# FFN entry: the rows of x turned by a product with a diagonal of the root, inside the last block of wo

## The chip, the cores and the metric

The kernel runs on one core of a Trainium2 chip. The metric is the device time of one execution in microseconds (us). The engines are named as in the profile: PE is TensorE (PEld its weight loads), DVE is VectorE, ACT is ScalarE, POOL is GpSimd, SP is SyncE, which issues every DMA here.

## The reference

One decoder layer on x of 256 tokens by 1024 channels, in float32. Three sub-layers follow each other, each wrapped in a norm before and a norm after:

```
h = rms_norm(x, norm_pre_xa)
y = cross_attention(h, rms_norm(mem, norm_mem), wq, wkv, wo)   # ends with o @ wo
x = x + rms_norm(y, norm_post_xa)
h = rms_norm(x, norm_pre_ffn)
y = (silu(h @ w_in[:, :2816]) * (h @ w_in[:, 2816:])) @ w_out
x = x + rms_norm(y, norm_post_ffn)
rms_norm(x, g) = x * rsqrt(mean(x * x) + 1e-6) * g             # mean over the 1024 channels
```

The change lies between `o @ wo` and the first products with the FFN's `w_in`.

## The kernel before

Float32 products with weights are made as three products each (`mm3`): an operand is split into a high part (rounded to a shorter format, written by ACT) and a rest (operand minus high, by DVE or POOL), and high by high, high by rest and rest by high are added up in one PSUM bank. Weights come in slots of 8 KB per partition; a slot is two halves, and half `i` is split by `high_part(act, i)` (ACT, line 344) and `rest(eng, e, i)` (DVE or POOL, line 350). A high part may be written only when the products with half `i - 4` are done, since there are four buffers for split halves. SP loads slot `n` when both rests of the slot that had its place before are made. On ACT, `highs(upto)` writes all high parts not yet written, up to half `upto - 1`; on DVE, `rests(upto)` does the same with rests. Before half `H_FIN` (the first FFN half, `first = 2 * S_FIN`) DVE makes all rests; from there on it makes the even halves, and POOL the odd ones. Below, "FFN half 0, 1, 2, 3" are `first` to `first + 3`: halves 0 and 1 are the gate's first 256 columns (channels 0 to 511, then 512 to 1023), halves 2 and 3 the up projection's.

Each engine works through its own instructions in the order of the program text, and semaphores tie them together. So the order of the calls in each engine's block is the order of the work.

wo is token-major (`split_token_major`): four PSUM banks, `wo0` and `wo1` for the first 128 tokens (block 0, columns 0 to 511 and 512 to 1023), `wo2` and `wo3` for the last 128 (block 1). Its 8 k-tiles are 8 weight halves, 12 products of 512 columns each. The first k-tiles run over all four banks; the last `last_kts` k-tiles run bank by bank, so that `wo0` is full first and `wo3` last.

For each block `m` of 128 tokens there follows a chain over three engines. ACT squares the two banks and makes the root (`post_root`), DVE multiplies the banks by the gain (`post_gain`) and adds them to x (`x_new`), ACT squares the new x and makes the root of the pre-norm (`pre_square`, `pre_part`, `pre_root`), DVE multiplies x by root and gain (`pre_norm`), PE turns the block by transposes (`turn_block`), and ACT and DVE split the turned block (`fft_high`, `fft_rest`). Then PE makes the first 256 gate and up columns block by block (`first_pair(m, e)`, where `e` is 0 for gate and 1 for up, 24 products each): turn 0, pair (0, gate), turn 1, pair (0, up), pair (1, gate), pair (1, up). After that come `g1`, `u1`, `g2` and so on for all 256 tokens at once, and the last product `y`.

The parts that the change touches, with what calls them:

Of the kernel before, what the change touches and what calls it, by code (L numbers as in the profile page):

```python
# [5 lines left out]
F32 = mybir.dt.float32  # L6
F32R = mybir.dt.float32r
ALU = mybir.AluOpType
# [72 lines left out]
H_WKV, H_LATE = 2 * S_WKV, 2 * S_WOUT  # L81
H_WQ, H_V7, H_WO, H_FIN = (2 * n for n in (S_WQ, S_V7, S_WO, S_FIN))
HALF_BUFS, MID_BUFS = 4, 2
Y_ORDER = [2, 3, 6, 7, 0, 1, 4, 5]

def trunk_kernel(nc, x_t, x_rows, mem_t, consts_d, params_d, weights_d, gains_d, rel_scratch, out):
    ctx = ExitStack()
    with ctx:  # L89
# [136 lines left out]
        act_split = [act_high, act_rest]  # L226
        fft = v3(own(ctx, "fft", 1024), 512)
        third_slot = own(ctx, "third_slot", SLOT)

# [3 lines left out]
        def cols(n):  # L233
# [22 lines left out]
            ml_row_step ml_den mb_inv s5_step2 rw_tail s5_sig x_inv f_sig s5_sq s5_root ml_sq  # L256
            ml_root rw_sq rw_root mb_sq mb_root
            w_high w_rest_even w_rest_odd w_rest_mid w_used high_ready act_rest y_rest h_high h_rest x_summed
# [108 lines left out]
        def _(pe):  # L367
# [46 lines left out]

            def split_token_major(first, tag, banks, act, order, last_kts, arrive, between=None):

# [19 lines left out]
                for m in range(2):  # L436
                    for half in range(2):
                        for kt in range(n - last_kts, n):
                            last = product(kt, m, half)
                            if m + half == 2 and kt < n - 1:  # L440
                                used(last, first + kt)
                        last.then_inc(full[banks[2 * m + half]], 1)
                half_user[first + n - 1] = f"{tag}3"
# [402 lines left out]

            split_token_major(2 * S_WO, "wo", (4, 5, 6, 7), ox_split, range(KD), 3, ox_arrives)

            def turn_block(m):

                for half in range(2):
                    i = 2 * m + half
                    o = v3(pe_open(pe, f"fft{i}", i)[:, :], P)
                    pe.wait_ge(S["xn_ready"], i + 1)
                    for k in range(4):
                        c = 4 * half + k
                        last = nc.tensor.transpose(o[:, k, :], xtmp[:, m, c * P:(c + 1) * P], const("ident"))
                    last.then_inc(full[i], 1)

            def first_pair(m, e):  # L860

                name = f"gu{m}"
                if e == 0:
                    pe_open(pe, name, 4 + m)
                o = bank[4 + m][:, 256 * e:256 * (e + 1)]
                for j in range(2):
# [11 lines left out]
                if e == 1:  # L878
# [82 lines left out]
        def _(pool):  # L961
# [76 lines left out]
            g.tensor_tensor(Sm[:, :, P:P + T], Sm[:, :, P:P + T], spread(mb_sum[:, 4:8], T), ALU.mult).then_inc(S["mb_prob"], 1)  # L1038
            for i in range(H_FIN + 1, NHALF, 2):
                rest(pool, g, i)  # L1040

        @block.scalar
        def _(act):
# [354 lines left out]
            pre_square(1, 0, 0)  # L1398
            pre_part(1, 0, 1.0 / D, "eps6")
            pre_square(1, 0, 1)  # L1400
            pre_root(1, 0, 1.0 / D)
            post_root(1, "wo", 1)
            highs(first + 2)

            def fft_high(m):
                for half in range(2):
                    o = v3(wait_full(act, f"fft{2 * m + half}")[:, :], P)
                    a.activation(h_split[0][:, 4 * half:4 * half + 4, m * P:(m + 1) * P], o,
                                 ACT.Copy).then_inc(S["high_ready"], 1)

            fft_high(0)
            pre_square(1, 1, 0)
            pre_part(1, 1, 1.0 / D, "eps6")
            pre_square(1, 1, 1)
            pre_root(1, 1, 1.0 / D)
            highs(first + 4)
            fft_high(1)

# [29 lines left out]
        def _(dve):  # L1448
# [10 lines left out]
            def rests(upto):  # L1459

                while split[0] < min(upto, NHALF):
                    if split[0] % 2 == 0 or split[0] < H_FIN:
                        rest(dve, v, split[0])
                    split[0] += 1
# [412 lines left out]

            def pre_norm(m):

                dve.wait_ge(S["pre_root"], 4 + 2 * m + 2)  # L1880
                for half in range(2):
                    cs = slice(half * 512, (half + 1) * 512)
                    dve.wait_ge(S["x_new"], 4 + 2 * m + half + 1)
                    v.scalar_tensor_tensor(xtmp[:, m, cs], xres[:, m, cs], rst_pre[:, m:m + 1], gain_pre[:, cs],
                                           ALU.mult, ALU.mult).then_inc(S["xn_ready"], 1)

# [57 lines left out]
            dve.wait_ge(S["gain_pre_in"], 16)  # L1944
            pre_norm(0)
            post_gain(1, "wo", 1, 1)
            x_new(1, "wo", 1)

            def fft_rest(m):
                for half in range(2):  # L1950
                    i = 2 * m + half
                    o = v3(wait_full(dve, f"fft{i}")[:, :], P)
                    high, rest_ = (x[:, 4 * half:4 * half + 4, m * P:(m + 1) * P] for x in h_split)
                    dve.wait_ge(S["high_ready"], HIGHS["fft"] + i + 1)
                    v.tensor_tensor(rest_, o, high.bitcast(F32), ALU.subtract).then_inc(free_of(f"fft{i}"), 1)

            fft_rest(0)
            pre_norm(1)
            rests(first + 4)
            fft_rest(1)  # L1960

# [187 lines left out]
```

## Time and profile before

| | |
|---|---|
| runs | 539.16, 537.88, 535.80 us; median 537.88 |
| the profiled execution | 536.21 us, span 534.4 us |
| mean granted clock of TensorE | 0.979 of full speed |
| busy: PE, DVE, ACT, POOL | 92%, 72%, 49%, 32% of the span |

The profiled execution is one run: its own time is 536.21 us, and its span, from the first to the last instruction in the trace, 534.4 us. All times of day below count from the span's start.
### The profile page before, as it was taken

How to read it: one execution, taken by the hardware profiler on the slowest of the kernel's cores; microseconds unless marked ns; L12 is line 12 of the kernel's file. 1: busy time of each engine (PE TensorE's matmuls, PEld its weight loads, DVE VectorE, ACT ScalarE, POOL GpSimd, SP SyncE). 2: the span in 40 equal slices, each digit the busy share in tenths (PEclk: the TensorE clock that was granted, in tenths of full speed). 3: DMA queues.
4: the chain of work that ended last, by engine and by line, in shares of the span. 5: the costliest groups of instructions: out<-in, count | busy, mean ns of one | idle time of the engine just before them, and what ended most of it. 6: DMA issues, size and time to landing. Idle time of an engine off the chain costs nothing.

```text
span 534.4 us, 8448 instructions
## 1 busy us (share of the span) xinstructions
PE 492.9 (92%) x3478; PEld 450.1 (84%) x3478; DVE 383.5 (72%) x443; ACT 261.5 (49%) x410; POOL 172.6 (32%) x103
## 2 busy tenths in 40 slices
PE   0799979999899998699999997799999999999986
PEld 0788969899698888588999986799999999988874
DVE  5676998699966966677946445689999999972114
ACT  3698782331522335356865536454444454443333
POOL 0130457466569512000000000353344344344440
PEclk9999998998899999899999999799999999999999
DMA  8847246112031122326473432436554455545602
GB/s 348 350 110 256 90 141 250 39 45 80 0 126 55 59 80 86 151 80 239 155 250 113 156 113 78 156 137 223 195 197 158 164 193 195 188 164 209 221 7 80
DMA packets 12358, 79.33 MB, mean 148 GB/s; under 512 B 1440, under 2 KB 2080, under 8 KB 3488
## 3 DMA queue, kind: packets, MB, share of 16 engines
q1 hardware_dynamic: 12320, 78.79, 41.7%
q8 instruction: 28, 0.46, 0.4%
q14 instruction: 10, 0.08, 0.0%
HBM read 76.95 MB, written 1.84 MB: 147 GB/s over the span
## 4 chain that ended last, share of the span: by engine, by line
PE 76%; DVE 10%; ACT 6%; issue 3%; DMA 3%; POOLq 0%; POOL 0%; SPq 0%; DVEq 0%; ACTq 0%
PE bank L369 75%; DMA vx<-mem_t 2%; DVE we_rest L350 2%; DVE vx L1689 2%; ACT we_high L344 1%; DMA ring<-weights 1%; ACT w_high L344 1%; DVE arena L1455 1%; ACT arena L1119 1%; DVE w_high L350 1%; DVE arena L1530 0%; ACT arena L1058 0%; DVE arena L1778 0%; POOLq L89 0%; POOL w_rest L350 0%
## 5 line engine op out<-in xcount | busy, mean ns | idle before, releaser
L344 ACT ACTIVATE w_high<-ring 128x1024 fp32r<-128x1024 f32 x70 | 73.7, 1058 | 81.6 <-PE bank L369 81.5
L369 PE MATMUL bank<-h_high,w_high 128*128 128x256 f32 x384 | 103.0, 284 | 0.0
L369 PE MATMUL bank<-h_rest,w_high 128*128 128x256 f32 x352 | 99.6, 283 | 0.0
L369 PE MATMUL bank<-h_high,w_rest 128*128 128x256 f32 x320 | 90.6, 283 | 0.0
L350 DVE TENSOR_TENSOR w_rest<-ring,w_high 128x1024 fp32r<-128x1024 f32 x42 | 53.5, 1277 | 42.4 <-ACT w_high L344 42.4
L350 POOL TENSOR_TENSOR w_rest<-ring,w_high 128x1024 fp32r<-128x1024 f32 x22 | 53.7, 2439 | 74.3 <-ACT w_high L344 74.3
L350 POOL TENSOR_TENSOR w_rest<-third_slot,w_high 128x1024 fp32r<-128x1024 f32 x11 | 26.5, 2407 | 154.1 <-ACT w_high L344 154.1
L369 PEld LDWEIGHTS bank<-h_high,w_high 128*128 128x128 f32 x384 | 71.7, 192 | 0.1
L369 PEld LDWEIGHTS bank<-h_rest,w_high 128*128 128x128 f32 x352 | 67.6, 192 | 0.0
L369 PEld LDWEIGHTS bank<-h_high,w_rest 128*128 128x128 f32 x320 | 61.4, 192 | 0.0
L369 PE MATMUL bank<-arena 128*128 128x128 f32 (+7 forms) x496 | 59.5, 302 | 1.5 <-ACT arena L1051 0.9
L369 PEld LDWEIGHTS bank<-arena 128*128 128x128 f32 (+3 forms) x496 | 52.8, 183 | 8.2 <-issue 2.8
L369 PE MATMUL bank<-h_high,we_high 128*128 128x256 f32 x128 | 38.9, 304 | 8.9 <-DVE h_rest L1486 5.6
L344 ACT ACTIVATE w_high<-third_slot 128x1024 fp32r<-128x1024 f32 x30 | 31.1, 1054 | 28.6 <-PE bank L369 28.6
L369 PE MATMUL bank<-h_high,we_rest 128*128 128x256 f32 x128 | 37.6, 294 | 0.0
L369 PE MATMUL bank<-h_rest,we_high 128*128 128x256 f32 x128 | 37.6, 294 | 0.0
L1455 DVE RECIPROCAL fft<-fft 128x512 f32<-128x512 f32 (+1 forms) x12 | 37.0, 3086 | 0.4
L350 DVE TENSOR_TENSOR w_rest<-third_slot,w_high 128x1024 fp32r<-128x1024 f32 x19 | 23.7, 1261 | 17.0 <-ACT w_high L344 17.0
L369 PE MATMUL bank<-w_high,act_high 128*128 128x512 f32 x88 | 34.5, 392 | 1.5 <-POOL w_rest L350 1.5
L369 PEld LDWEIGHTS bank<-h_high,we_high 128*128 128x128 f32 x128 | 26.1, 204 | 10.8 <-issue 7.1
L369 PE MATMUL bank<-w_rest,act_high 128*128 128x512 f32 x88 | 34.3, 389 | 0.0
L369 PE MATMUL bank<-w_high,act_rest 128*128 128x512 f32 x88 | 34.3, 389 | 0.0
(308 smaller groups left out, 1236.8 us busy)
## 6 DMA issues: line engine op xcount, KB each, us to landing
ring<-weights SPq DMA_DIRECT2D x50, 1024.0 KB, 4.9
third_slot<-weights SPq DMA_DIRECT2D x15, 1024.0 KB, 4.9
cst<-consts SPq DMA_DIRECT2D x1, 1664.0 KB, 12.1
gain<-gains SPq DMA_DIRECT2D x3, 512.0 KB, 5.8
par<-params SPq DMA_DIRECT2D x1, 1168.0 KB, 14.4
kx<-x_t SPq DMA_DIRECT2D x1, 1024.0 KB, 4.9
vx<-mem_t SPq DMA_DIRECT2D x1, 1024.0 KB, 10.2
xres<-x_rows SPq DMA_DIRECT2D x1, 1024.0 KB, 8.7
```

The source lines that it names most:

```text
L344: nc.scalar.activation(split_half(i)[0], raw_half(i), ACT.Copy).then_inc(S["w_high"], 1)
L350: e.tensor_tensor(rest_, raw_half(i), high.bitcast(F32), ALU.subtract).then_inc(rest_done(i)[0], 1)
L369: return nc.tensor.matmul(out_, lhsT, rhs, start=start, stop=stop, skip_group_check=True)
L1119: e = a.activation(sin[:, i, :], const("time"), ACT.Copy, scale=frac[:, i:i + 1])
L1455: return v.reciprocal(x, x)
L1689: last = v.scalar_tensor_tensor(mem_h[:, k, :], mem_h[:, k, :], prm("norm_mem")[:, k:k + 1], rstd_m, ALU.mult, ALU.mult)
```

## The change

The root of the FFN's pre-norm is no longer multiplied into x by DVE. DVE multiplies by the gain alone (`pre_gain`). ACT makes a diagonal matrix of the root (`fft_diag`: the identity times the root of each row, into a free part of `fft`), and PE turns and scales the block in one float32 product with it. `turn_block(0)` is called from inside wo, in bank `wo3`, ahead of its last k-tile. wo ends with four k-tiles bank by bank rather than three. `first_pair(0, 1)` is cut in two, and `turn_block(1)` stands between its parts. DVE makes the rests of FFN halves 0 to 3; POOL starts with half 5. The order on ACT and on DVE is new.

```diff
@@ H_POOL = H_FIN + 4
+diag = v3(fft[:, 1, 0:2 * P], P)
@@ split_token_major(..., at_end=None), the part bank by bank
                             if m + half == 2 and kt < n - 1:
                                 used(last, first + kt)
+                            if m + half == 2 and kt == n - 2 and at_end:
+                                at_end()
@@ tensor
-            split_token_major(2 * S_WO, "wo", (4, 5, 6, 7), ox_split, range(KD), 3, ox_arrives)
@@ turn_block(m)
                     pe.wait_ge(S["xn_ready"], i + 1)
+                    pe.wait_ge(S["diag_ready"], m + 1)
                     for k in range(4):
                         c = 4 * half + k
-                        last = nc.tensor.transpose(o[:, k, :], xtmp[:, m, c * P:(c + 1) * P], const("ident"))
+                        last = mm(o[:, k, :], xtmp[:, m, c * P:(c + 1) * P], diag[:, m, :])
+            split_token_major(2 * S_WO, "wo", (4, 5, 6, 7), ox_split, range(KD), 4, ox_arrives,
+                              at_end=lambda: turn_block(0))
-            turn_block(0)
             first_pair(0, 0)
+            first_pair(0, 1, (0,))
             turn_block(1)
-            first_pair(0, 1)
+            first_pair(0, 1, (1,))
             first_pair(1, 0)
             first_pair(1, 1)
@@ gpsimd
-            for i in range(H_FIN + 1, NHALF, 2):
+            for i in range(H_POOL + 1, NHALF, 2):
@@ scalar
+            def fft_diag(m):
+                act.wait_ge(S["pre_root"], 4 + 2 * m + 2)
+                a.activation(diag[:, m, :], const("ident"), ACT.Copy, scale=rst_pre[:, m:m + 1]).then_inc(S["diag_ready"], 1)
+            highs(first)
+            post_root(1, "wo", 0)
+            pre_block(0)               # pre_square, pre_part, pre_square, pre_root, fft_diag
             highs(first + 1)
-            post_root(1, "wo", 0)
-            (pre_square ... pre_root of block 0)
+            fft_high(0)                # one half of a block now
+            fft_high(1)
             post_root(1, "wo", 1)
             highs(first + 2)
-            fft_high(0)
-            (pre_square ... pre_root of block 1)
+            pre_block(1)
             highs(first + 4)
-            fft_high(1)
+            fft_high(2)
+            fft_high(3)
@@ vector
-            rests(first + 1)
+            rests(first)
             dve.wait_ge(S["gain_in"], 32)
             post_gain(1, "wo", 0, 0)
             post_gain(1, "wo", 0, 1)
             x_new(1, "wo", 0)
+            dve.wait_ge(S["gain_pre_in"], 16)
+            pre_gain(0)
             post_gain(1, "wo", 1, 0)
-            pre_norm(0)
+            rests(first + 1)
+            fft_rest(0)
+            fft_rest(1)
             post_gain(1, "wo", 1, 1)
+            rests(first + 2)
             x_new(1, "wo", 1)
-            fft_rest(0)
-            pre_norm(1)
+            pre_gain(1)
             rests(first + 4)
-            fft_rest(1)
+            fft_rest(2)
+            fft_rest(3)
```

## Rows read from the trace of the kernel before

**Rows 1.** The page, part 4: the chain that ended last, by engine.

```profile
PE 76%; DVE 10%; ACT 6%; issue 3%; DMA 3%; POOLq 0%; POOL 0%; SPq 0%; DVEq 0%; ACTq 0%
```

**Rows 2.** Timeline of TensorE: start, length, engine and line, operation, count, [idle before].

```profile
320.76 0.39 PE L369 MATMUL bank<-w_high,ox_high 128*128 128x512 f32 x1
...
323.93 0.39 PE L369 MATMUL bank<-w_high,ox_rest 128*128 128x512 f32 x1
...
325.29 0.39 PE L369 MATMUL bank<-w_high,ox_rest 128*128 128x512 f32 x1
...
332.15 1.29 PE L857 MATMUL bank<-cst,xtmp 128*128 128x128 f32 x8 [2.40 <-DVE xtmp L1884]
337.41 0.55 PE L369 MATMUL bank<-w_high,h_high 128*128 128x256 f32 x1 [3.96 <-DVE h_rest L1955]
...
341.88 1.04 PE L857 MATMUL bank<-cst,xtmp 128*128 128x128 f32 x8
...
351.40 0.28 PE L369 MATMUL bank<-h_high,w_high 128*128 128x256 f32 x1
```

**Rows 3.** Timeline of ScalarE from wo to the first FFN pair.

```profile
318.92 1.06 ACT L344 ACTIVATE w_high<-ring 128x1024 fp32r<-128x1024 f32 x1 [1.60 <-PE bank L369]
...
325.72 0.60 ACT L1308 ACTIVATE px<-bank 128x512 f32<-128x512 f32 x1 [1.02 <-PE bank L369]
...
329.85 0.20 ACT L1346 ACTIVATE small<-small 128x1 f32<-128x1 f32 x1
329.95 0.58 ACT L1308 ACTIVATE px<-bank 128x512 f32<-128x512 f32 x1
...
332.94 1.14 ACT L1408 ACTIVATE h_high<-bank 128x512 fp32r<-128x512 f32 x2
...
351.88 2.00 ACT L344 ACTIVATE w_high<-third_slot 128x1024 fp32r<-128x1024 f32 x2
```

**Rows 4.** Timeline of VectorE over the same stretch.

```profile
320.01 1.23 DVE L350 TENSOR_TENSOR w_rest<-ring,w_high 128x1024 fp32r<-128x1024 f32 x1 [1.44 <-ACT w_high L344]
...
327.05 1.40 DVE L1875 SCALAR_TENSOR_TENSOR xres<-xtmp,small,xres 128x512 f32<-128x512 f32 x2
330.66 0.69 DVE L1867 TENSOR_TENSOR xtmp<-bank,gain 128x512 f32<-128x512 f32 x1 [2.21 <-ACT px L1308]
...
333.19 3.48 DVE L1875 SCALAR_TENSOR_TENSOR xres<-xtmp,small,xres 128x512 f32<-128x512 f32 x2
...
339.62 1.22 DVE L350 TENSOR_TENSOR w_rest<-ring,w_high 128x1024 fp32r<-128x1024 f32 x1
```

**Rows 5.** Windows: length, busy (and count) of PE, PEld, DVE, ACT, POOL, TensorE's granted clock, DMA.

```profile
333.50:334.00 0.50, 0.00 (x0) 0.00 (x0) 0.50 (x1) 0.50 (x2) 0.50 (x1) 1.00 0.00 0
334.50:335.00 0.50, 0.00 (x0) 0.00 (x0) 0.50 (x1) 0.00 (x0) 0.50 (x1) 0.50 0.00 0
...
341.00:341.50 0.50, 0.50 (x6) 0.50 (x5) 0.00 (x0) 0.00 (x0) 0.50 (x1) 1.00 0.00 0
```

**Rows 6.** Timeline of TensorE: products of plain float32 operands, 128 and 256 columns.

```profile
164.88 5.34 PE L369 MATMUL bank<-arena 128*128 128x128 f32 x48
...
300.81 7.15 PE L369 MATMUL bank<-ptx,vx 128*128 128x256 f32 x32
```

**Rows 7.** Groups by line and shape, whole run: count | busy us, mean ns | idle before.

```profile
L1241 ACT ACTIVATE arena<-arena,small 128x128 f32<-128x128 f32 x4 | 1.6, 389 | 0.0
...
L1834 DVE TENSOR_TENSOR arena<-arena 128x512 f32<-128x512 f32 x1 | 0.7, 691 | 0.0
...
L1453 DVE TENSOR_SCALAR fft<-fft 128x512 f32<-128x512 f32 x10 | 22.5, 2250 | 4.4 <-ACT fft L1439 4.4
```

**Rows 8.** Timeline of GpSimd: its first rest.

```profile
333.11 2.34 POOL L350 TENSOR_TENSOR w_rest<-third_slot,w_high 128x1024 fp32r<-128x1024 f32 x1 [121.70 <-ACT w_high L344]
```

**Rows 9.** Timeline of SyncE's queue: the weight load after FFN halves 0 and 1.

```profile
335.53 0.33 SPq L943 DMA_DIRECT2D third_slot<-weights  x1
```

**Rows 10.** The page, part 6: DMA issues, KB each, us to landing.

```profile
third_slot<-weights SPq DMA_DIRECT2D x15, 1024.0 KB, 4.9
```

More of the change, by code:

```diff
@@ L82 @@
 H_WQ, H_V7, H_WO, H_FIN = (2 * n for n in (S_WQ, S_V7, S_WO, S_FIN))
+H_POOL = H_FIN + 4
 HALF_BUFS, MID_BUFS = 4, 2
@@ L256, in trunk_kernel @@
             ml_row_step ml_den mb_inv s5_step2 rw_tail s5_sig x_inv f_sig s5_sq s5_root ml_sq
-            ml_root rw_sq rw_root mb_sq mb_root
+            ml_root rw_sq rw_root mb_sq mb_root diag_ready
             w_high w_rest_even w_rest_odd w_rest_mid w_used high_ready act_rest y_rest h_high h_rest x_summed
@@ L413, in split_values, with split_token_major @@
                     used(last, i, name if j else None)
-            def split_token_major(first, tag, banks, act, order, last_kts, arrive, between=None):
+            def split_token_major(first, tag, banks, act, order, last_kts, arrive, between=None, at_end=None):
                 ys = [pe_open(pe, f"{tag}{i}", b) for i, b in enumerate(banks)]
@@ L854, in turn_block, with first_pair @@
                     pe.wait_ge(S["xn_ready"], i + 1)
+                    pe.wait_ge(S["diag_ready"], m + 1)
                     for k in range(4):
                         c = 4 * half + k
-                        last = nc.tensor.transpose(o[:, k, :], xtmp[:, m, c * P:(c + 1) * P], const("ident"))
+                        last = mm(o[:, k, :], xtmp[:, m, c * P:(c + 1) * P], diag[:, m, :])
                     last.then_inc(full[i], 1)
-            def first_pair(m, e):
+            split_token_major(2 * S_WO, "wo", (4, 5, 6, 7), ox_split, range(KD), 4, ox_arrives,
+                              at_end=lambda: turn_block(0))
+            def first_pair(m, e, parts=(0, 1)):
                 name = f"gu{m}"
-                if e == 0:
+                if e + parts[0] == 0:
                     pe_open(pe, name, 4 + m)
                 o = bank[4 + m][:, 256 * e:256 * (e + 1)]
-                for j in range(2):
+                for j in parts:
                     i = 2 * (S_FIN + e) + j
@@ L877, in first_pair @@
                         used(last, i)
-                if e == 1:
+                if e + parts[-1] == 2:
                     last.then_inc(full[4 + m], 1)
@@ L1395, in _, with fft_high, pre_block @@
             first = 2 * S_FIN
-            highs(first + 1)
-            post_root(1, "wo", 0)
[L1398 to L1401, printed above, removed]
+            def fft_diag(m):
+                act.wait_ge(S["pre_root"], 4 + 2 * m + 2)
+                a.activation(diag[:, m, :], const("ident"), ACT.Copy, scale=rst_pre[:, m:m + 1]).then_inc(S["diag_ready"], 1)
+            def fft_high(i):
+                m, half = i // 2, i % 2
+                o = v3(wait_full(act, f"fft{i}")[:, :], P)
+                a.activation(h_split[0][:, 4 * half:4 * half + 4, m * P:(m + 1) * P], o,
+                             ACT.Copy).then_inc(S["high_ready"], 1)
+            def pre_block(m):
+                pre_square(1, m, 0)
+                pre_part(1, m, 1.0 / D, "eps6")
+                pre_square(1, m, 1)
+                pre_root(1, m, 1.0 / D)
+                fft_diag(m)
+            highs(first)
+            post_root(1, "wo", 0)
+            pre_block(0)
+            highs(first + 1)
+            fft_high(0)
+            fft_high(1)
             post_root(1, "wo", 1)
             highs(first + 2)
[L1405 to L1409, printed above, removed]
-            fft_high(0)
[L1412 to L1415, printed above, removed]
+            pre_block(1)
             highs(first + 4)
-            fft_high(1)
+            fft_high(2)
+            fft_high(3)
             def act_high(p):
@@ L1461, in rests @@
                 while split[0] < min(upto, NHALF):
-                    if split[0] % 2 == 0 or split[0] < H_FIN:
+                    if split[0] % 2 == 0 or split[0] < H_POOL:
                         rest(dve, v, split[0])
@@ L1876, in x_new, with pre_gain @@
                                            ALU.add).then_inc(S["x_new"], 1)
-            def pre_norm(m):
-                dve.wait_ge(S["pre_root"], 4 + 2 * m + 2)
+            def pre_gain(m):
                 for half in range(2):
@@ L1883, in pre_norm @@
                     dve.wait_ge(S["x_new"], 4 + 2 * m + half + 1)
-                    v.scalar_tensor_tensor(xtmp[:, m, cs], xres[:, m, cs], rst_pre[:, m:m + 1], gain_pre[:, cs],
-                                           ALU.mult, ALU.mult).then_inc(S["xn_ready"], 1)
+                    v.tensor_tensor(xtmp[:, m, cs], xres[:, m, cs], gain_pre[:, cs], ALU.mult).then_inc(S["xn_ready"], 1)
             def rest_of_bank(tag, i, out, high, scale=None):
@@ L1937, in _, with fft_rest @@
             first = 2 * S_FIN
-            rests(first + 1)
+            def fft_rest(i):
+                m, half = i // 2, i % 2
+                o = v3(wait_full(dve, f"fft{i}")[:, :], P)
+                high, rest_ = (x[:, 4 * half:4 * half + 4, m * P:(m + 1) * P] for x in h_split)
+                dve.wait_ge(S["high_ready"], HIGHS["fft"] + i + 1)
+                v.tensor_tensor(rest_, o, high.bitcast(F32), ALU.subtract).then_inc(free_of(f"fft{i}"), 1)
+            rests(first)
             dve.wait_ge(S["gain_in"], 32)
@@ L1942, in _ @@
             x_new(1, "wo", 0)
+            dve.wait_ge(S["gain_pre_in"], 16)
+            pre_gain(0)
             post_gain(1, "wo", 1, 0)
-            dve.wait_ge(S["gain_pre_in"], 16)
-            pre_norm(0)
+            rests(first + 1)
+            fft_rest(0)
+            fft_rest(1)
             post_gain(1, "wo", 1, 1)
+            rests(first + 2)
             x_new(1, "wo", 1)
[L1949 to L1955, printed above, removed]
-            fft_rest(0)
-            pre_norm(1)
+            pre_gain(1)
             rests(first + 4)
-            fft_rest(1)
+            fft_rest(2)
+            fft_rest(3)
             def act_rest(p):
```

## The prediction

> **What bounds the kernel now.** I read the page's chain first: TensorE holds 76% of what ended last [rows 1], so a change counts by how much earlier or later TensorE gets through. Then TensorE's timeline between wo and `g1`, for its idle time. It waits twice: 2.40 us for the normed rows of block 0 ahead of the first turn, and 3.96 us between that turn and the first gate products, until block 0 is split [rows 2]. The windows show a third loss. The granted clock, 1.00 until 334, is 0.50 in the second wait and 1.00 again at 341 [rows 5]. From 337.41 to 341.88 stand 24 products of 256 columns, 4.47 us; the 8 transposes from 341.88 (0.87 us by the second turn's 1.04 less some 0.17 of drain) and the next 72 products reach to 351.40, which is 0.12 us each [rows 2]. So the 24 would have taken 2.88, and the low clock costs 1.6 us. In all some 8 us lie here. After 351.40, where `g1` starts, TensorE has no wait until the last stage, and VectorE waits for ScalarE's exponential once in each of the ten pairs (4.4 us in sum, [rows 7]), so it keeps pace. Therefore one question decides: when does `g1` start?
>
> **The first block.** The last four k-tiles now run bank by bank, so `wo0` asks for k-tile 7 already as its tenth product there, where the 58th product of wo stood (320.76, [rows 2]). But the rest of that half runs on VectorE from 320.01 to 321.24, since its high part could start only at 318.92, when k-tile 3 was done [rows 3, 4]. It was covered by k-tile 4 before. With 0.14 us from rest to product (what lies between VectorE and TensorE at 337.41), the wait is 0.62, and I add 0.13 for the restart: 0.75 us. Bounds 0.6 and 0.9. Against it, `wo1` is full with the 72nd product and not the 78th: 325.29 less 323.93 is 1.36 earlier [rows 2]. The square of `wo1` starts at 325.72 - 1.36 + 0.75 = 325.11, and the chain of block 0 is 0.61 us early. The pre-root ended at 330.05 [rows 3], now 329.44. The diagonal comes behind it: a scaled 128x128 on ScalarE took 0.389 us [rows 7], bounds 0.2 (the 128x1 at 329.85, [rows 3]) and 0.5. Ready at 329.85, turn at 329.98. VectorE's product with the gain is off the path: the sum is early by 0.61 too, ends near 327.8 (327.05 + 1.40 - 0.61, [rows 4]), and two multiplications of 0.691 [rows 7] end before the diagonal. The product ahead of the turn is the 93rd, 15 behind the one at 325.29: it starts at 325.29 + 15 x 0.227 + 0.75 = 329.44 and is through at 329.67, so TensorE waits 0.3.
>
> **The turn as a product.** Sixteen plain float32 products of 256 columns stand in the trace as 32 instructions in 7.15 us, so a product is two; at 128 columns an instruction is 5.34 / 48 = 0.11 us [rows 6]. Eight products are 16 x 0.11 = 1.76 us for the 0.87 of the transposes. I take 1.76; the lower bound is 0.87, the upper one 3.5 at the low clock. With the drain the first block is turned at 332.0. Here stands a rule against the change. The Trainium skill, "TensorE: Matmul & The Clock Gate", Terms, says that the transpose mode is 4 times faster for float32. By it a turn would be 3.5 us; by the rows it is twice the transposes, and the rows are of this kernel.
>
> **The order behind it.** This is the part that decides. ScalarE now does `fft_high(0)`, `fft_high(1)` and only then the squares of `wo2`, which before ran at 329.95, ahead of the split [rows 3]. The second high ends at 332.0 + 0.57 (half of 1.14, [rows 3]) = 332.57. VectorE's `post_gain` of `wo2` stood 0.71 us behind the start of that square (330.66 and 329.95, [rows 3, 4]), so it now starts at 333.3; and `post_gain` stands ahead of FFN half 0's rest and of `fft_rest(0)` in VectorE's queue. What is queued behind this wait, by start-to-start distances (0.6 us for a 512, 1.15 for a rest, as 1.22 less the overlap of neighbours, [rows 4]): `post_gain` 333.3, rest of half 0 333.9, `fft_rest(0)` 335.05, `fft_rest(1)` 335.65, `post_gain` of `wo3` 336.25, rest of half 1 336.85, `x_new(1)` 338.0. TensorE starts the gate products at 335.05 + 0.68 + 0.14 = 335.87 (337.41 before), with 12 of them, and takes half 1 at 336.85 + 1.23 + 0.14 = 338.2. So far the change is ahead by about 1 us.
>
> Then it loses. ScalarE writes the high parts of halves 2 and 3 behind `pre_block(1)`, which waits for `x_new(1)`. From the start of `x_new` to the end of the pre-root it took 327.05 to 330.05, 3.00 us [rows 3, 4]: 341.0. Diagonal: 341.4. High of half 2 (1.06, [rows 3]): 342.45. Rest on VectorE: 343.7. TensorE: 343.85. Its 12 products of half 1 ended at 338.2 + 1.45 = 339.65, so a new wait of 4.2 us opens in front of half 2; in the kernel before this rest ran at 339.62, on time [rows 4]. What POOL's absence gives is in this sum already: `x_new(1)` took 3.48 us beside POOL's rest of half 1 and 1.40 alone [rows 4, 8], 2.1 us on VectorE, but two more rests of 1.15 there eat it.
>
> From 343.85: 12 products, 1.44 and 0.1 of restart; turn of block 1, 1.76 (diagonal at 341.4 and `pre_gain` by 340.7 don't hold it); half 3 with 12 (its rest is made at 344.9); 48 for block 1. That is 343.85 + 1.54 + 1.76 + 60 x 0.12 = 354.35 for the start of `g1`, 2.95 us later than 351.40. Block 1 is split under the 12 products of half 3: the second turned half is there at 347.3, its high and rest take 0.57 + 0.68, to 348.6, and TensorE needs it at 348.6. No cover is left there, so up to 0.3 us can be added.
>
> **The clock.** In the kernel before it went to 1.2 GHz after 2.40 us idle, 1.29 us of transposes and 0.5 us idle, and rose some 3.4 us after products ran again [rows 2, 5]. The new wait of 4.2 us is longer than either of these. I expect the clock at 1.2 GHz when it ends, and the same price as before, 1.6 us. The low clock around 336 to 339 costs nothing now, since half 1's rest is what TensorE waits for. Bounds of this term: 0 and 2.4 (half 2's products, the turn and half 3's at half speed for longer). The skill's same page, in Part 4: PE-mode transpose, says that transposes don't count as work for the clock; by that the products in the turn would hold it up through the first wait. It changes nothing in the sum, which prices that wait's clock at nothing, but it is a reason for the case without the 1.6.
>
> **Elsewhere.** The slot of halves 0 and 1 is free at 338.1 and not at 335.45, so SyncE issues the load 2.6 us later than 335.53 [rows 9]; it lands 4.9 us on [rows 10], 343.0, and its first high is at 351.88 [rows 3]. Hidden, with 8.9 us to spare. POOL's first rest is now half 5, as late against `g1` as before. Nothing moves in the FFN itself.
>
> **Sum.** 536.21 + 2.95 + 1.6 = 540.8 us against the profiled execution's own time (the 1.8 us around its span stay). The median of the runs shown is 1.67 above that execution; I set the base halfway, at 537.0, and forecast 541.6.
>
> **Rivals.**
> - The wait opens and the clock stays high, or falls so late that it costs little: 537.0 + 2.95 = 540.0. For it speaks that the products of half 1 run just ahead of the wait.
> - The wait does not open (the other side). Place: half 2's rest in front of `first_pair(0, 1, (0,))`. If it is there when TensorE comes at 339.65, 4.2 us and the clock's 1.6 are saved: 537.0 + 2.95 - 4.2 = 535.8, faster. From `x_new(1)`'s start to TensorE's start are 5.85 us, so `x_new(1)` must start by 333.8. The root that it needs ends 2.15 us behind the square of `wo2` at 332.57, so 334.7: against it stand both the root and three rests in VectorE's queue. It would need ScalarE to square `wo2` ahead of the turned halves.
> - The turn is dearer. Two turns at 3.5 us add 2 x 1.74 = 3.5: 545.1. This is what the quoted factor of 4 gives; against it speak the 0.11 us of 48 instructions [rows 6].
> - It doesn't do what it says: the turn is not hidden in `wo3`, since the diagonal is late by more (dearer diagonal, longer stall at k-tile 7). Then TensorE stands in front of the turn, the last 3 products of `wo3` are queued behind, and everything above slides by that much: up to 0.8 us, 542.4.
>
> **How the numbers follow.** Chances: likeliest 0.58, clock stays high 0.22, turn not hidden 0.10, turn dearer 0.04, wait does not open 0.06. Low end: the case without clock cost, less the cheap bound of a turn (0.9) and 1.0 for the base (own time against median), 538.2. High end: the likeliest with the clock's upper bound (0.8), 0.3 for block 1's split, 0.6 for stall and diagonal, and a base higher by 0.7, 544.0. A measurement of this kernel can tell about 1% (5.4 us) from no change. Slower by more than that, over 543.3, needs the dear turn or most upper bounds at once: 0.18. Faster by more needs all that lies here: 0.03. The rest, 0.79.
>
> **What the profile will show.** Right: a 0.6 us wait in wo at about 320.8; 16 instructions of the turn at 330.0, 3 products of wo behind them; the gate at 335.9; a wait of 3 to 4.5 us on half 2's rest, ending near 343.9; clock 0.50 behind it; `g1` at 354 to 356. Wrong: `x_new(1)` of block 1 well before 338, no wait ahead of half 2, or a turn of other than 1.8 us.

## The result, and the profile after

The changed kernel takes 540.88 us (median of 7 runs, 540.39 to 543.15), the kernel before 538.73 (7 runs, 535.80 to 539.58): ratio 1.0064, with a 95% interval of 1.0035 to 1.0092. It is slower, by 0.6%, which lies inside the forecast's range and on its side. The two medians differ by 2.15 us; the ratio weighs all runs and puts the difference at 3.4 us, with an interval of 1.9 to 5.0. The profiled execution of the changed kernel took 542.93 us, span 541.1.

The two profiled executions don't start wo at the same time, though the code ahead of it is the same: wo's first product starts at 307.62 in the trace of before and at 310.01 in this one. So I compare what follows from that product on. "Stretch" below is the time from wo's first product to the first product of `g1`: 351.40 - 307.62 = 43.78 us before, 358.11 - 310.01 = 48.10 us now, 4.32 us more. From `g1` to the end both need 183.0 us. So behind wo's first product these two executions differ in the stretch alone.

Timeline of TensorE in the changed kernel, from the stall in wo to `g1` (start, length, engine and line, operation, count, [idle before]); it answers to [rows 2]:

```profile
322.94 0.39 PE L371 MATMUL bank<-w_high,ox_rest 128*128 128x512 f32 x1
323.70 0.50 PE L371 MATMUL bank<-w_high,ox_high 128*128 128x512 f32 x1 [0.37 <-DVE w_rest L352]
...
332.34 2.02 PE L371 MATMUL bank<-fft,xtmp 128*128 128x128 f32 x16 [0.19 <-ACT fft L1406]
334.12 0.48 PE L371 MATMUL bank<-w_high,ox_high 128*128 128x512 f32 x1
...
338.18 0.55 PE L371 MATMUL bank<-w_high,h_high 128*128 128x256 f32 x1 [3.11 <-DVE h_rest L1957]
...
345.97 0.39 PE L371 MATMUL bank<-w_high,h_high 128*128 128x256 f32 x1 [2.34 <-DVE w_rest L352]
...
347.57 3.50 PE L371 MATMUL bank<-fft,xtmp 128*128 128x128 f32 x16
350.83 0.36 PE L371 MATMUL bank<-w_high,h_high 128*128 128x256 f32 x1
...
358.11 0.28 PE L371 MATMUL bank<-h_high,w_high 128*128 128x256 f32 x1
```

The first turn is where the change wants it, inside wo, and the wait in front of it is down from 2.40 us [rows 2] to 0.19. The gate (the first product with `h_high`, at 338.18) starts 28.17 us behind wo's first product; before it was 29.79. So far 1.6 us are won. Then TensorE waits 2.34 us for half 2's rest, until 345.97, and the second turn takes 347.57 to 350.83, 3.26 us, where the first took 332.34 to 334.12, 1.78.

Timeline of ScalarE, the same kernel: the diagonal of block 0, the high of half 0, the two highs of the turned block, the square of `wo2`, then what comes behind `x_new(1)`; it answers to [rows 3]:

```profile
331.80 0.40 ACT L1406 ACTIVATE fft<-cst,small 128x128 f32<-128x128 f32 x1
332.11 1.04 ACT L346 ACTIVATE w_high<-third_slot 128x1024 fp32r<-128x1024 f32 x1
333.51 0.60 ACT L1411 ACTIVATE h_high<-bank 128x512 fp32r<-128x512 f32 x1 [0.36 <-PE bank L371]
334.40 0.60 ACT L1411 ACTIVATE h_high<-bank 128x512 fp32r<-128x512 f32 x1 [0.30 <-PE bank L371]
334.90 0.59 ACT L1314 ACTIVATE px<-bank 128x512 f32<-128x512 f32 x1
...
341.06 0.63 ACT L1336 ACTIVATE px<-xres 128x512 f32<-128x512 f32 x1 [3.07 <-DVE xres L1890]
...
343.62 1.99 ACT L346 ACTIVATE w_high<-ring 128x1024 fp32r<-128x1024 f32 x2
```

Timeline of VectorE; it answers to [rows 4]:

```profile
335.61 0.69 DVE L1882 TENSOR_TENSOR xtmp<-bank,gain 128x512 f32<-128x512 f32 x1 [4.24 <-ACT px L1314]
336.22 1.22 DVE L352 TENSOR_TENSOR w_rest<-third_slot,w_high 128x1024 fp32r<-128x1024 f32 x1
337.35 1.28 DVE L1957 TENSOR_TENSOR h_rest<-bank,h_high 128x512 fp32r<-128x512 f32 x2
...
339.15 1.22 DVE L352 TENSOR_TENSOR w_rest<-third_slot,w_high 128x1024 fp32r<-128x1024 f32 x1
340.28 1.41 DVE L1890 SCALAR_TENSOR_TENSOR xres<-xtmp,small,xres 128x512 f32<-128x512 f32 x2
...
344.69 2.36 DVE L352 TENSOR_TENSOR w_rest<-ring,w_high 128x1024 fp32r<-128x1024 f32 x2 [1.80 <-ACT w_high L346]
```

Read the two together. VectorE idles 4.24 us for one square (334.90) that stands behind two highs of the turned block. Behind that wait it works without a break from 335.61 to the sum of block 1 at 340.28. ScalarE in turn idles 3.07 us for that sum, and only then, at 343.62, comes to the highs of halves 2 and 3. Their inputs were ready long before: where these highs stand ahead of `pre_block(1)` (highs first, below), ScalarE starts them 27.87 us behind wo's first product, here 33.61. TensorE's wait in front of 345.97 is the end of this chain.

Windows of the same kernel (length; busy and count of PE, PEld, DVE, ACT, POOL; TensorE's granted clock; DMA); they answer to [rows 5]:

```profile
336.00:337.00 1.00, 0.00 (x0) 0.00 (x0) 1.00 (x2) 0.94 (x5) 0.00 (x0) 1.00 0.00 0
...
340.00:341.00 1.00, 1.00 (x7) 1.00 (x6) 1.00 (x3) 0.00 (x0) 0.00 (x0) 0.50 0.00 0
...
344.00:345.00 1.00, 0.00 (x0) 0.00 (x0) 0.31 (x1) 1.00 (x2) 0.00 (x0) 1.00 0.49 205
...
346.50:347.00 0.50, 0.50 (x6) 0.50 (x6) 0.50 (x1) 0.00 (x0) 0.00 (x0) 1.00 0.00 0
...
348.00:349.00 1.00, 1.00 (x6) 1.00 (x6) 0.00 (x0) 0.00 (x0) 0.00 (x0) 0.50 0.93 172
...
351.00:352.00 1.00, 1.00 (x11) 1.00 (x10) 0.19 (x1) 0.60 (x1) 0.00 (x0) 1.00 0.26 107
```

The clock went to 1.2 GHz (0.50) twice. The first time it fell between 337 and 338, inside the wait in front of the gate, and it was back at 1.00 while TensorE waited for half 2. The second time it fell about 1.4 us after the products of half 2 had started (between 347.0 and 347.5), and was back before 351. The first low stretch slows products whose delay ends in a wait anyway, the second slows the turn, which is on the path.

### The profile page after: what moved, and what is told of

It reads as the page before. It is cut to its first block, busy times and chain, and to the rows that moved or that the text cites. A ratio compares the mean times of both kernels' runs of the same rounds, so it can differ in the third digit from the quotient of the medians.

```text
span 541.1 us, 8481 instructions
## 1 busy us (share of the span) xinstructions
PE 499.6 (92%) x3494; PEld 455.4 (84%) x3494; DVE 384.4 (71%) x445; ACT 262.3 (48%) x412; POOL 167.3 (31%) x101
## 4 chain that ended last, share of the span: by engine, by line
PE 75%; DVE 11%; ACT 6%; issue 3%; DMA 3%; POOLq 0%; POOL 0%; SPq 0%; DVEq 0%; ACTq 0%
PE bank L371 74%; DMA vx<-mem_t 2%; DVE we_rest L352 2%; DVE vx L1704 2%; DMA ring<-weights 1%; ACT we_high L346 1%; DVE w_rest L352 1%; ACT w_high L346 1%; DVE arena L1470 1%; ACT arena L1125 1%; DVE w_high L352 1%; DVE arena L1545 0%; DVE arena L1793 0%; ACT arena L1064 0%; POOLq L90 0%
## 5 line engine op out<-in xcount | busy, mean ns | idle before, releaser
L352 POOL TENSOR_TENSOR w_rest<-ring,w_high 128x1024 fp32r<-128x1024 f32 x21 | 50.8, 2419 | 206.3 <-ACT w_high L346 206.3
L352 DVE TENSOR_TENSOR w_rest<-ring,w_high 128x1024 fp32r<-128x1024 f32 x43 | 54.7, 1277 | 44.2 <-ACT w_high L346 44.2
L352 DVE TENSOR_TENSOR w_rest<-third_slot,w_high 128x1024 fp32r<-128x1024 f32 x20 | 24.9, 1259 | 15.5 <-ACT w_high L346 15.4
L352 POOL TENSOR_TENSOR w_rest<-third_slot,w_high 128x1024 fp32r<-128x1024 f32 x10 | 24.1, 2412 | 32.4 <-ACT w_high L346 32.4
```

Of the source, the lines that this page charges most:

```text
L352: e.tensor_tensor(rest_, raw_half(i), high.bitcast(F32), ALU.subtract).then_inc(rest_done(i)[0], 1)
```

## The experiments

Each of the ten experiments tests one or more explanations of the loss. Theory A says that the order on ScalarE and VectorE costs the time: the square of `wo2` behind the turned block's highs, and the highs of halves 2 and 3 behind `pre_block(1)`. Rival B is the turn as a product, rival C the stall at k-tile 7 with the four k-tiles by block, rival D the rests that VectorE took over from POOL.

The table has the total, and three marks and the stretch of the profiled execution, counted from wo's first product. "First turn", "gate" and "half 2" are the starts of the first turn, of the first gate product and of the first product with half 2. Each ratio is against runs of the kernel before on the same chip at about the same time; their medians were 538.05 us for the first four experiments told below, 538.65 for the next four and 537.87 for the last two. Executions with the same code ahead of wo start it up to 4.4 us apart (see the end), so the stretch is the finer measure. It comes from one execution of each kernel, so how far it varies for one kernel isn't measured. Marks that kernels should share agree to 0.05 us: the first turn at 22.30 to 22.33 in six kernels, half 2 at 35.92 to 35.96 in three. The stretch less that of before lies in the interval of the total's difference in all but one kernel (squares first: 3.6 us by the stretch, 1.4 to 3.1 by the total).

| kernel | median us | ratio to before (interval) | first turn | gate | half 2 | stretch |
|---|---|---|---|---|---|---|
| before | 538.73 | 1 | 24.53 | 29.79 | | 43.78 |
| the change | 540.88 | 1.0064 (1.0035 to 1.0092) | 22.33 | 28.17 | 35.96 | 48.10 |
| squares first | 539.93 | 1.0042 (1.0025 to 1.0058) | 22.30 | 26.01 | 34.13 | 47.38 |
| highs first | 539.13 | 1.0022 (1.0000 to 1.0045) | 22.33 | 28.16 | no wait | 44.08 |
| both orders | 535.48 | 0.9959 (0.9941 to 0.9978) | 22.30 | 26.01 | 31.03 | 41.54 |
| transposes again | 540.33 | 1.0050 (1.0026 to 1.0073) | 22.76 | 27.86 | 35.60 | 46.80 |
| three k-tiles | 543.92 | 1.0111 (1.0063 to 1.0160) | 23.01 | 28.85 | 36.64 | 48.72 |
| turn after wo | 541.54 | 1.0074 (1.0050 to 1.0098) | 22.67 | 28.43 | 36.22 | 48.31 |
| POOL odd halves | 541.32 | 1.0065 (1.0032 to 1.0098) | 22.33 | 28.17 | 35.92 | 48.06 |
| both orders, transposes | 534.65 | 0.9942 (0.9910 to 0.9974) | 22.75 | 25.75 | 30.75 | 41.09 |
| fillers | 542.05 | 1.0068 (1.0033 to 1.0104) | 22.32 | 28.16 | 35.96 | 46.47 |
| the same, turn after wo | 534.90 | 0.9956 (0.9930 to 0.9981) | 22.74 | 25.73 | 30.53 | 40.86 |

### ScalarE's square of wo2 ahead of the turned block's highs

`post_root` is cut: `post_first` is its first square with the small part, and the last argument leaves it out of `post_root`.

```diff
             pre_block(0)
+            post_first(1, "wo", 1)
             highs(first + 1)
             fft_high(0)
             fft_high(1)
-            post_root(1, "wo", 1)
+            post_root(1, "wo", 1, False)
             highs(first + 2)
             pre_block(1)
```

> Only ScalarE's order is changed: the square of wo2 and its small part stand ahead of the two highs of the turned block. Measure: from wo's first product to g1's first product, 43.8 us in the trace of before and 48.1 in that of the change. Theory A (order: squares of wo2 queued behind the turned halves hold VectorE, and the highs of halves 2 and 3 are queued behind pre_block(1)): VectorE's post_gain of wo2 starts within 1 us of the diagonal, the wait on half 2's rest shrinks by 1.5 us, stretch 46.6 us. Rival B (the turn as a product is what costs): 48.1, no change. Rival C (the stall at k-tile 7 and four k-tiles by block): 48.1.

VectorE in this kernel:

```profile
330.57 0.69 DVE L1888 TENSOR_TENSOR xtmp<-bank,gain 128x512 f32<-128x512 f32 x1 [1.44 <-ACT px L1314]
331.85 1.23 DVE L352 TENSOR_TENSOR w_rest<-third_slot,w_high 128x1024 fp32r<-128x1024 f32 x1 [0.58 <-ACT w_high L346]
```

Its wait for the square is 1.44 us and not 4.24; the gate starts 2.2 us earlier and half 2 1.8 us earlier than in the change. The stretch is shorter by 0.7 only, and not by 1.5. The rest went to the clock: between half 2's first product and `g1` lie 47.38 - 34.13 = 13.25 us here, 12.14 in the change and, with the clock held (fillers, below), 10.51. So the low clock cost 2.7 us in this run and 1.6 in the change. Here it fell inside the wait and was low under all of half 2's first products and the turn (TensorE, then a window):

```profile
341.94 0.58 PE L371 MATMUL bank<-w_high,h_high 128*128 128x256 f32 x1 [3.87 <-DVE w_rest L352]
...
344.67 3.49 PE L371 MATMUL bank<-fft,xtmp 128*128 128x128 f32 x16
```

```profile
342.00:344.50 2.50, 2.50 (x12) 2.50 (x13) 1.02 (x1) 0.00 (x0) 0.00 (x0) 0.50 0.29 36
```

The total is also lower than the change's, but the two intervals overlap. Theory A holds so far that the order matters; rivals B and C, which left it no effect, can't be the whole cause.

One part of the expectation failed. The wait on half 2's rest did not shrink by 1.5 us, it grew from 2.34 to 3.87. With the short wait in front of the gate (0.99) the clock stayed at 1.00 there, so TensorE was through with half 1 sooner and stood longer in front of half 2.

### The highs of halves 2 and 3 ahead of pre_block(1)

```diff
             post_root(1, "wo", 1)
-            highs(first + 2)
-            pre_block(1)
             highs(first + 4)
+            pre_block(1)
@@ vector
             x_new(1, "wo", 1)
+            rests(first + 3)
             pre_gain(1)
             rests(first + 4)
```

> Only the highs of halves 2 and 3 are put ahead of pre_block(1) on ScalarE, and on VectorE half 2's rest ahead of the gain of block 1. Theory A: the wait ahead of half 2 goes (rest made some 3.2 us earlier), and the products run on; stretch 44.2 us if the clock is low in the first pair, 43.2 if it is not. Rivals B and C: 47 or more, since turn and stall stay.

Measured 44.08, as expected for a low clock in the first pair (the granted clock was 0.50 from 340 to 345). TensorE has no wait in front of half 2: the rest is made from 343.55, and the products run through from the gate at 340.12 to the turn.

```profile
340.12 0.55 PE L371 MATMUL bank<-w_high,h_high 128*128 128x256 f32 x1 [3.11 <-DVE h_rest L1956]
...
347.06 1.95 PE L371 MATMUL bank<-fft,xtmp 128*128 128x128 f32 x16
```

That alone takes back 4.0 of the 4.3 us. The total agrees: 1.0022, with an interval that reaches down to 1.0000.

### Both orders

The two edits together.

> Both orders together, all else as in the change. Theory A: first gate product 1.5 to 2 us earlier than in the change, half 2 without a wait of over 1 us, stretch 42.3 us with the clock held and 43.9 with one fall; total below that of the kernel before by 0 to 1.5 us, and 4 to 6 below the change. Rivals B and C: still slower than before by 1 us or more, since product and stall are both in it.

TensorE and VectorE in this kernel:

```profile
335.77 0.36 PE L371 MATMUL bank<-w_high,h_high 128*128 128x256 f32 x1 [0.98 <-DVE h_rest L1962]
...
338.33 0.39 PE L371 MATMUL bank<-w_high,h_high 128*128 128x256 f32 x1 [0.90 <-DVE w_rest L352]
...
340.79 0.39 PE L371 MATMUL bank<-w_high,h_high 128*128 128x256 f32 x1 [0.76 <-DVE w_rest L352]
```

```profile
338.19 1.41 DVE L1895 SCALAR_TENSOR_TENSOR xres<-xtmp,small,xres 128x512 f32<-128x512 f32 x2
339.52 1.22 DVE L352 TENSOR_TENSOR w_rest<-ring,w_high 128x1024 fp32r<-128x1024 f32 x1
```

A window over the second half of the stretch, with the columns as above:

```profile
330.00:352.00 22.00, 19.17 (x146) 17.68 (x145) 16.31 (x22) 15.36 (x34) 2.24 (x1) 1.00 0.27 96
```

Three waits of under 1 us are left, all on VectorE. The clock stayed at 1.00 through the stretch, which is 41.54 us. With its product, its stall and all that the change has added, the kernel is now faster than the one before: 0.9959, interval 0.9941 to 0.9978. So neither the product nor the four k-tiles makes the kernel slower than before once the order is right; the order is worth 6.6 us of stretch (48.10 - 41.54). I had expected 42.3 with the clock held, and a total 0 to 1.5 us below the kernel before; the medians differ by 2.6.

### The turn by transposes again

VectorE multiplies by root and gain behind the root, as before the change; the diagonal is gone.

```diff
-                    pe.wait_ge(S["diag_ready"], m + 1)
-                        last = mm(o[:, k, :], xtmp[:, m, c * P:(c + 1) * P], diag[:, m, :])
+                        last = nc.tensor.transpose(o[:, k, :], xtmp[:, m, c * P:(c + 1) * P], const("ident"))
-                fft_diag(m)
@@ pre_gain(m)
+                dve.wait_ge(S["pre_root"], 4 + 2 * m + 2)
-                    v.tensor_tensor(xtmp[:, m, cs], xres[:, m, cs], gain_pre[:, cs], ALU.mult)
+                    v.scalar_tensor_tensor(xtmp[:, m, cs], xres[:, m, cs], rst_pre[:, m:m + 1], gain_pre[:, cs], ALU.mult, ALU.mult)
```

> The product with the diagonal is undone alone: VectorE multiplies by root and gain behind the root, TensorE turns by transposes, all orders as in the change. Theory A: each turn 0.87 us instead of 1.76, given back in part by VectorE's multiplication behind the root; stretch 46.5 to 47.2 us, the wait on half 2's rest still 3 us or more. Rival B: the whole loss goes, stretch 44 or less.

Measured 46.80. TensorE in this kernel:

```profile
330.34 1.29 PE L859 MATMUL bank<-cst,xtmp 128*128 128x128 f32 x8 [0.60 <-DVE xtmp L1892]
331.39 0.48 PE L371 MATMUL bank<-w_high,ox_high 128*128 128x512 f32 x1
```

A turn takes 1.05 us to the next product, where the product with the diagonal takes 1.78; the turn starts 0.4 us later, for VectorE's multiplication. In the stretch the product costs 1.3 us of the change's 4.3: 0.3 up to half 2, the rest behind it, where the second turn runs at the low clock. The other 3.0 us of the loss stay without it, so rival B, by which the whole loss would go, falls. The expectation's wait of 3 us or more in front of half 2 was not met: it is 2.28.

This run also says how little the diagonal itself brings forward. Even with transposes the first turn starts at 22.76, against 24.53 in the kernel before: 1.77 us earlier. The diagonal adds 0.43 to that. Of the 1.77, 0.7 come with the fourth k-tile (next experiment). The remaining 1.1 fits the new order on VectorE, where block 0's normed rows no longer stand behind the gain of `wo2`; no run isolates it.

### Three k-tiles by block, the turn after wo, POOL for the odd halves

```diff
-            split_token_major(2 * S_WO, "wo", (4, 5, 6, 7), ox_split, range(KD), 4, ox_arrives,
+            split_token_major(2 * S_WO, "wo", (4, 5, 6, 7), ox_split, range(KD), 3, ox_arrives,
```

> wo ends with three k-tiles by block again, all else as in the change (the turn stays inside wo3). The wait of TensorE at k-tile 7 goes (0.6 us and a restart), but wo1 is full 1.36 us later against the rest of wo. Theory A: the chain of block 0 starts 0.6 us later and all behind it with it; TensorE stands 1 us or more in front of the turn; stretch from wo's first to g1's first product 0.6 us longer than the change's at the same clock, 48.7. Rival C (the stall is what costs): 0.7 us shorter, 47.4.

Measured 48.72. The stall at k-tile 7 is gone, and TensorE waits 1.55 us for the diagonal instead of 0.19:

```profile
331.23 2.02 PE L371 MATMUL bank<-fft,xtmp 128*128 128x128 f32 x16 [1.55 <-ACT fft L1406]
```

The gate and half 2 are 0.7 us later. The fourth k-tile is worth its stall; rival C falls. The total (4 runs) has too wide an interval to tell this kernel from the change.

```diff
-            split_token_major(2 * S_WO, "wo", (4, 5, 6, 7), ox_split, range(KD), 4, ox_arrives,
-                              at_end=lambda: turn_block(0))
+            split_token_major(2 * S_WO, "wo", (4, 5, 6, 7), ox_split, range(KD), 4, ox_arrives)
+            turn_block(0)
```

> turn_block(0) behind wo3's last products and not ahead of its last k-tile, all else as in the change. Theory A: the three products of wo (0.7 us) run while TensorE would wait for the diagonal (0.2 us), so the turn starts 0.4 to 0.5 us later and everything behind it with it; stretch 48.5 us at the same clock. Rival (hiding the turn is worth the turn): 1.8 us longer, 49.9.

Measured 48.31; the turn starts 0.34 us later, half 2 0.26 us later. The place inside wo is worth 0.3 us at the turn and 0.2 in the stretch: the diagonal holds the turn back inside wo (0.19 us of wait in the change), so little is left to win.

```diff
-H_POOL = H_FIN + 4
+H_POOL = H_FIN
```

> POOL makes the rests of halves 1 and 3 again (H_POOL = H_FIN), all else as in the change. Theory A: half 1's rest takes 2.35 us on POOL instead of 1.23 behind VectorE's queue and ends at about the same time; x_new(1) starts 1.2 us earlier on VectorE but lies beside POOL's rest and takes that much longer; half 2's rest comes as late as in the change within 0.5 us; stretch 47.6 to 48.6 us at the same clock. Rival D (the rests taken over by VectorE are what delays x_new(1)): 1.2 us shorter or more, 46.9.

Measured 48.06, half 2 at 35.92. VectorE, the sum of block 1 beside POOL's rest of half 1, which ran from 338.92 for 2.37 us:

```profile
340.01 2.50 DVE L1890 SCALAR_TENSOR_TENSOR xres<-xtmp,small,xres 128x512 f32<-128x512 f32 x2
```

Counted from wo's first product it starts at 29.14, 1.13 us earlier than in the change, and takes 2.50 us instead of 1.41. It ends at the same time. Who makes the odd rests makes no difference in this kernel, and rival D falls.

### Both orders with transposes

The edits of the third and the fourth kernel together.

> Both orders as in the third run, but the turn by transposes and the root multiplied in by VectorE. Theory A: where the order is right, the product with the diagonal is worth little: the first turn starts 0.35 us later and is 0.9 us shorter, behind it VectorE's queue decides; the second turn starts as early, since half 2's products cover the wait for the root; stretch 41.0 to 41.6 us against 41.5. Rival B (the product's 0.9 us per turn lies on the path): 39.8.

Measured 41.09, 0.45 us less than with the product; in total 0.9942 (0.9910 to 0.9974) against 0.9959 (0.9941 to 0.9978), which the totals can't tell apart. In the right order the product with the diagonal gives nothing over the transposes, and by the stretch of one execution each it costs 0.45 us. So what the title names is not what makes these kernels faster than the one before.

### Products that keep TensorE busy in its waits

These products' results are read by nobody; nothing else of the change is touched.

```diff
+            def fill(n):
+                for _ in range(n):
+                    mm(bank[3][:, 0:256], const("ident"), cst[:, CONST["ident"][0]:CONST["ident"][0] + 256])
+
+            fill(6)
             first_pair(0, 0)
+            fill(8)
             first_pair(0, 1, (0,))
             turn_block(1)
```

> The change, with products whose result nobody reads in TensorE's two waits: 6 float32 products of 256 columns (2.7 us) ahead of the first gate products and 8 (3.6 us) ahead of half 2. They end before the rests that TensorE waits for, so they only keep it busy. Theory A's clock term: the clock stays at 1.00, the second turn takes 1.8 us instead of 3.3, stretch from wo's first to g1's first product 46.6 us instead of 48.1, with half 2 as late as in the change. Rival (the second turn is slow for another reason, such as its operands, or the wait is longer than the products): 48 us or more.

TensorE in this kernel:

```profile
335.96 2.75 PE L371 MATMUL bank<-cst 128*128 128x256 f32 x12
339.24 0.36 PE L371 MATMUL bank<-w_high,h_high 128*128 128x256 f32 x1 [0.53 <-DVE h_rest L1963]
...
343.02 3.62 PE L371 MATMUL bank<-cst 128*128 128x256 f32 x16
347.04 0.39 PE L371 MATMUL bank<-w_high,h_high 128*128 128x256 f32 x1 [0.41 <-DVE w_rest L352]
...
348.57 1.95 PE L371 MATMUL bank<-fft,xtmp 128*128 128x128 f32 x16
350.28 0.36 PE L371 MATMUL bank<-w_high,h_high 128*128 128x256 f32 x1
```

Gate and half 2 start exactly when they do in the change (28.16 and 35.96), the clock is 1.00 throughout, the second turn takes 348.57 to 350.28, 1.71 us, and the stretch is 46.47: 1.63 us less than the change, and this is the clock's share of the loss. The total, 1.0068 (1.0033 to 1.0104), doesn't show this gain: its interval reaches 0.35% either way, and 1.6 us are 0.3%. That the whole kernel gains by it is not shown.

### The fastest without the call inside wo

```diff
 (both orders, transposes)
-                              at_end=lambda: turn_block(0))
+            turn_block(0)
```

> Both orders, transposes, and the first turn behind wo, no call inside wo3. Theory A: in the kernel with both orders and transposes TensorE waited 0.6 us in front of the turn, and the three products of wo that are now ahead of it take 0.7, so the turn starts 0.1 us later and all behind it stands on VectorE's queue; stretch 41.1 to 41.3 us against 41.1. Rival (the place inside wo3 is what gives the gain over the kernel before): 42 us or more.

Measured 40.86, and 0.9956 (0.9930 to 0.9981). That is a little below the 41.1 to 41.3 expected. The turn starts at the same time (22.74 and 22.75), and the last three products of wo no longer stand behind it. The gain over the kernel before does not come from the place inside wo, nor from the product. What is left in this kernel is the fourth k-tile, the order on ScalarE and VectorE, the cut of `first_pair(0, 1)` and the odd rests on VectorE. How its 2.9 us of stretch divide between them was not measured, beyond the fourth k-tile's 0.7 in the change.

## Why the prediction was right

Forecast 541.6 us, measured 540.88. The sum put the change at 4.55 us; the stretch of the two profiled executions says 4.32, the totals 3.4 (by the ratio) or 2.15 (by the medians). That the forecast's total is off by only 0.7 is in part luck: its base of 537.0 was 1.7 below the median that the kernel before then had, 538.73. The side and the cause were right. Two things came out right by other ways than forecast: the clock, and how the wait in front of half 2 was made up. Step by step, in times from wo's first product (307.62 taken off the forecast):

- **The stall at k-tile 7.** 0.75 expected. TensorE's start went from 322.94 + 0.23 = 323.17 to 323.70, and the restart cost 0.1: 0.63 us. That the fourth k-tile is worth more than its stall followed from 1.36 less 0.75; undoing it made half 2 0.7 us later.
- **Diagonal and turn.** Turn at 22.36 expected, 22.33 measured; the diagonal took 0.40 (0.389 from the row), the turn 1.78 (1.76). The wait in front of it was 0.19 instead of 0.3. The Trainium skill's factor of 4 for the transpose mode in float32 ("TensorE: Matmul & The Clock Gate", Terms) is not what this kernel shows. A second turn, start to start at the full clock between products of 256 columns, took 1.71 us as a product (fillers) and 342.68 - 341.88 = 0.80 by transposes (before, [rows 2] and the line here), a factor of 2.1.

```profile
342.68 0.37 PE L369 MATMUL bank<-w_high,h_high 128*128 128x256 f32 x1
```

- **The order.** Gate at 28.25 expected, 28.17 measured; half 2 at 36.23 expected, 35.96 measured. The order experiments show that this is the cause and not only a chain that fits: each part of the order undone alone brought half 2 forward or removed its wait, and with both undone all the rest of the change is a gain.
- **The wait in front of half 2.** Forecast as 4.2 us (3 to 4.5 in the signs), measured as 2.34. The end was right and the beginning wrong: the first pair ran at the low clock and ended 1.6 us later than forecast, inside the wait. The prediction had priced that clock at nothing, and so it was: the fillers kept it up and half 2 came at 35.96 all the same. But its reason was another one. It had TensorE waiting for half 1's rest; at the low clock there is no such wait in the trace, and it is half 2's wait that takes up the delay.
- **The clock.** 1.6 us expected, 1.63 by the fillers, and that they agree so well is luck. The prediction had the clock at 1.2 GHz when the wait ends. In the trace it was at 1.00 then and fell about 1.4 us later, so the turn paid and half 2's first 12 products hardly did. In the kernel with the squares first the clock was low when the wait ended, as forecast, and that cost 2.7, above the upper bound of 2.4. The Trainium skill's rule that transposes don't count as work for the clock (same page, Part 4: PE-mode transpose) is neither borne out nor refuted: the clock fell in the wait behind the first turn with the product (the change) and with transposes (transposes again) alike, so the product in the turn did not hold it up through the first wait; and it stayed up through waits of at most 1 us with products (both orders) and at most 1.71 us with transposes (the last kernel).
- **POOL.** Taken as a draw, and a draw it is: with POOL the sum of block 1 starts 1.13 us earlier and takes 1.09 us longer.
- **The load behind halves 0 and 1.** Expected 2.6 us later and hidden. SyncE issued it at 340.44, 30.43 us behind wo's first product, against 27.91 before: 2.5 us later. From `g1` on nothing changed.
- **The low end of the range.** Its terms add up to 538.1, and not to 538.2.
- **The other side.** The wait does not open only if ScalarE squares `wo2` ahead of the turned halves, the text said. This was too narrow. Moving the highs of halves 2 and 3 alone closed the wait too; I had looked for what could make `x_new(1)` early, and not at the highs, which don't need `x_new(1)` and were only queued behind it. And squares first alone, which met that condition, left a wait of 3.87 us. That the case would be faster than before was right for both orders together (0.9959).

## What to carry to other kernels

Where engines work through fixed queues, price a move by what stands behind the moved wait on its own engine. Here the first turn came 2.2 us earlier. One square put behind the turned block's highs cost VectorE 4.2 us of waiting, and two weight highs put behind `pre_block(1)` cost the stretch 4.0 us; both undone gave 6.6. Work whose inputs are ready (the weight highs here) is better placed ahead of an instruction that waits for a chain, where it fits into that wait. And a wait of TensorE can have a second price, in the low clock of what follows it: 1.6 and 2.7 us in two kernels here.

## What the runs showed of the hardware

Executions of the same code ahead of wo differ by as much as the change is worth. In twelve profiled executions wo's first product starts between 307.6 and 312.0 us. Their granted clock ahead of wo differs too. Here are windows over the same times of the kernel before and of the one with the highs first, with the columns as above:

```profile
60.00:90.00 30.00, 26.85 (x191) 23.62 (x190) 27.18 (x43) 18.38 (x29) 19.42 (x17) 0.94 0.50 169
120.00:150.00 30.00, 27.48 (x197) 24.79 (x196) 26.10 (x35) 10.46 (x14) 18.13 (x11) 0.89 0.19 64
```

```profile
60.00:90.00 30.00, 26.85 (x182) 23.83 (x181) 26.30 (x42) 17.46 (x29) 19.24 (x17) 0.89 0.50 168
120.00:150.00 30.00, 26.14 (x179) 22.48 (x177) 27.42 (x37) 9.78 (x14) 16.16 (x10) 0.83 0.14 46
```

The second got 0.05 to 0.06 less clock in both, and in these 60 us it started 27 fewer products (361 against 388). That the clock makes the whole difference of 4.3 us is not shown. With 4 to 12 runs of a kernel the intervals of the totals reach 0.2 to 0.5% either way, so a total hardly resolves 2 us here; the marks inside the stretch repeat to 0.05 us.

A wait of the same length does not always bring the clock down. In the change TensorE waits 3.11 us for the gate's first product and goes on at 1.2 GHz. With three k-tiles it waits 3.11 us in the same place, having waited 1.55 us in front of the turn too, and goes on at 2.4 GHz (TensorE, then a window):

```profile
337.07 0.35 PE L371 MATMUL bank<-w_high,h_high 128*128 128x256 f32 x1 [3.11 <-DVE h_rest L1957]
```

```profile
337.50:338.50 1.00, 1.00 (x11) 1.00 (x9) 1.00 (x3) 0.00 (x0) 0.00 (x0) 1.00 0.00 0
```
